# Weighted sum of gathered expert rows: from TensorE products with diagonals to scaled additions on VectorE

## What is computed

```
q  = (hx @ wq)                                   # 8 heads x 2 halves x 64
s1, s2 = scores of both halves against 128 keys each; top 16 of each; best 16 of the 256 sums
gate = softmax over the 16 chosen of a head
eid  = index of the chosen expert rows
act  = gelu(einsum('td,thkd->thk', hx, u[eid]))   # one dot product per slot
out  = einsum('thk,thkd->td', gate * act, v[eid]) # weighted sum of 128 rows of V per token
```

## Time and profile before

| what | us |
|---|---|
| median of 3 runs | 5882.7 (5859.87 to 5891.56) |
| span of the profiled execution, first to last instruction | 5620.3 |
| what lies around the span, median less span | 262.4 |
| five pair passes, first gather issue to the end of the last add to X | 743.4, 736.6, 736.2, 749.2, 739.1 |
| busy in the span: TensorE | 4119.9 (73%) |
| busy: VectorE | 3021.2 (54%) |
| busy: ScalarE | 954.0 (17%) |
| busy: GpSimd | 3143.7 (56%) |

### The profile page before, as it was taken

The page is one execution under the profiler, slowest core; times in us unless marked ns, Lnnn a source line. Parts: engine busy times, 40 slices in busy tenths (PEclk is TensorE's granted clock), DMA queues, the critical chain, the costliest instruction groups (busy, mean ns, idle before and its releaser), DMA issues. The chain is left out here.

```text
span 5620.3 us, 37241 instructions
## 1 busy us (share of the span) xinstructions
PE 4119.9 (73%) x10909; PEld 1832.8 (33%) x10909; DVE 3021.2 (54%) x6541; ACT 954.0 (17%) x2298; POOL 3143.7 (56%) x2740
## 2 busy tenths in 40 slices
PE   7986777677776677775778779677846777576766
PEld 2533554322222222322223235345512222222222
DVE  1129652765663765655646521575366466465663
ACT  0012350111111111111111110234011111111111
POOL 0005302377776777776777730240167777677775
PEclk9998898899999899998999999789979999899999
DMA  7100101499998999998999951011179999899998
GB/s 274 53 16 8 18 25 64 153 383 368 395 364 346 386 372 398 389 376 326 379 396 390 365 190 60 8 17 41 42 264 355 378 362 364 316 370 365 381 355 337
DMA packets 459025, 1468.37 MB, mean 261 GB/s; under 512 B 58966, under 2 KB 97066, under 8 KB 458818
## 3 DMA queue, kind: packets, MB, share of 16 engines
q0 software_dynamic: 368640, 1342.34, 62.7%
q1 hardware_dynamic: 81548, 116.43, 6.3%
q10 hardware_dynamic: 8634, 7.14, 0.4%
HBM read 1459.62 MB, written 6.13 MB: 261 GB/s over the span
## 5 line engine op out<-in xcount | busy, mean ns | idle before, releaser
L1530 PE MATMUL tile_acc<-peer_V,peer_diag 128*128 128x512 f32 x5120 | 2490.5, 622 | 736.6 <-DMA peer_V<-in_peer_v_dram,peer_expert 695.8
L1551 DVE CUSTOM_DVE_ANT_0 peer_U<-peer_U,peer_h 128x1024 f32<-128x1024 f32 x1280 | 1543.8, 1225 | 1377.8 <-DMA peer_U<-in_peer_u_dram,peer_expert 1373.1
L1463 POOL DMA_INDIRECT peer_U<-in_peer_u_dram,peer_expert x1280 | 1389.4, 1085 | 643.5 <-issue 526.3
L1469 POOL DMA_INDIRECT peer_V<-in_peer_v_dram,peer_expert x1280 | 1446.3, 1130 | 402.9 <-issue 271.4
L1530 PEld LDWEIGHTS tile_acc<-peer_V,peer_diag 128*128 128x128 f32 x5120 | 923.4, 195 | 2282.3 <-issue 1441.4
L1505 ACT ACTIVATE peer_diag<-small,peer_w 128x128 f32<-128x128 f32 x1280 | 493.0, 401 | 2365.2 <-PE tile_acc L1530 2139.2
L338 PE MATMUL proj_acc<-proj_w,HT 128*128 128x512 f32 (+2 forms) x1280 | 481.7, 538 | 2.9 <-DVE PR L366 2.9
L1348 PE MATMUL tile_keys<-peer_sub,peer_q 64*128 64x128 f32 x320 | 46.5, 435 | 374.8 <-DVE peer_rest L1364 294.2
L338 PEld LDWEIGHTS proj_acc<-proj_w,HT 128*128 128x128 f32 x1280 | 242.8, 190 | 235.0 <-issue 217.4
L660 POOL MEMSET glascore_Q<- 128x8192 f32 x2 | 13.8, 6925 | 539.7 <-POOLq L100 539.7
L1200 POOL TENSOR_TENSOR X<-X,out_part 128x512 f32<-128x512 f32 x20 | 25.3, 1266 | 470.6 <-DVE out_part L1190 470.6
(11 more groups left out here) (250 smaller groups left out, 3381.2 us busy)
## 6 DMA issues: line engine op xcount, KB each, us to landing
setup_ada<-in_ada_w_dram SPq DMA_DIRECT2D x12, 2048.0 KB, 16.9
peer_ada<-in_ada_w_dram SPq DMA_DIRECT2D x24, 1024.0 KB, 12.5
proj_w<-in_w_in_dram SPq DMA_DIRECT2D x10, 2048.0 KB, 7.9
peer_U<-in_peer_u_dram,peer_expert POOLq DMA_INDIRECT x1280, 6.5
peer_V<-in_peer_v_dram,peer_expert POOLq DMA_INDIRECT x1280, 6.6
out_w<-in_w_out_dram SPq DMA_DIRECT2D x2, 4096.0 KB, 14.9
query_w<-in_peer_wq_dram SPq DMA_DIRECT2D x4, 2048.0 KB, 16.0
Y<-mods SPq DMA_DIRECT2D x8, 512.0 KB, 7.4
```

The lines of the kernel that those rows point to most:

```text
L1463: pool.indirect_dma_start(s.U[:, n % RING], None, u_rows, bass.IndirectOffsetOnAxis(ap=s.expert[:, n // SLOTS, n % SLOTS:n % SLOTS + 1], a ...
L1469: pool.indirect_dma_start(s.V[:, n % RING], None, v_rows, bass.IndirectOffsetOnAxis(ap=s.expert[:, n // SLOTS, n % SLOTS:n % SLOTS + 1], a ...
L1530: mm = nc.tensor.matmul(acc[:, n // SLOTS, half], s.diag[:, n % 4], s.V[:, n % RING, 512 * half:512 * half + 512], start=n % SLOTS == 0, s ...
L1551: nc.vector.tensor_tensor_reduce(out=s.U[:, n % RING], in0=s.U[:, n % RING], in1=s.h[:, n // SLOTS], scale=1.0, scalar=0.0, op0=ALU.mult, ...
```

## The change

The sum over slots is made on VectorE in SBUF. Behind the dot product of slot n stands a scaled addition for slot n - 16: `part_out = V row * weight + part_out`, with a plain scaling for the first slot of a tile. VectorE waits for each one to end before it goes on. TensorE's products, ScalarE's diagonals and the PSUM sum are gone. `add_out` now reads the SBUF sum, and the one of the first tile comes a head earlier (head 8), as the sum's only buffer is needed again from head 9. GpSimd's order and its waits have the same text, but `sums` now counts scaled additions. VectorE's loop has a round more, for the last 16.

```diff
-        s.diag = sb("diag", [P, 4, P])
...
-            acc = st.ps("acc", [P, 2, 2, 512])
...
                     for h in range(NH + 1):
                         if h % PH == PH // 2 + 1:
                             softmax_exp(nc, act, s, sems, h // PH)
-                        if h:
-                            act.wait_ge(weights, h)
-                            for n in range((h - 1) * TOPK, h * TOPK):
-                                if n >= 4:
-                                    act.wait_ge(sums, n - 3)
-                                nc.scalar.activation(s.diag[:, n % 4], m.ident, ACT.Copy, scale=s.w[:, n:n + 1]).then_inc(diags, 1)
...
-                        if h:
-                            for n in range((h - 1) * TOPK, h * TOPK):
-                                pe.wait_ge(diags, n + 1)
-                                pe.wait_ge(vg[n % RING], 16 * (n // RING + 1))
-                                for half in range(2):
-                                    mm = nc.tensor.matmul(acc[:, n // SLOTS, half], s.diag[:, n % 4],
-                                                          s.V[:, n % RING, 512 * half:512 * half + 512],
-                                                          start=n % SLOTS == 0, stop=n % SLOTS == SLOTS - 1)
-                                mm.then_inc(sums, 1)
...
+                    def weigh_row(n):
+
+                        dve.wait_ge(vg[n % RING], 16 * (n // RING + 1))
+                        dve.wait_ge(weights, n // TOPK + 1)
+                        if n % SLOTS == 0:
+                            nc.vector.tensor_scalar(s.part_out[:], s.V[:, n % RING], s.w[:, n:n + 1], None, ALU.mult).then_inc(sums, 1)
+                        else:
+                            nc.vector.scalar_tensor_tensor(out=s.part_out[:], in0=s.V[:, n % RING], scalar=s.w[:, n:n + 1],
+                                                           in1=s.part_out[:], op0=ALU.mult, op1=ALU.add).then_inc(sums, 1)
+                        dve.wait_ge(sums, n + 1)
+
                     def add_out(j):
 
-                        dve.wait_ge(sums, SLOTS * (j + 1))
-                        link(nc.vector.tensor_tensor(s.part_out[:], acc[:, j].rearrange("p a b -> p (a b)"), s.G[:], ALU.mult))
+                        link(nc.vector.tensor_tensor(s.part_out[:], s.part_out[:], s.G[:], ALU.mult))
...
-                    for h in range(NH):
+                    for h in range(NH + 1):
                         for k in range(TOPK):
                             n = h * TOPK + k
-                            dve.wait_ge(ug[n % RING], 16 * (n // RING + 1))
-                            nc.vector.tensor_tensor_reduce(out=s.U[:, n % RING], in0=s.U[:, n % RING], in1=s.h[:, n // SLOTS],
-                                                           scale=1.0, scalar=0.0, op0=ALU.mult, op1=ALU.add,
-                                                           accum_out=s.dots[:, n:n + 1]).then_inc(dots, 1)
+                            if h < NH:
+                                dve.wait_ge(ug[n % RING], 16 * (n // RING + 1))
+                                nc.vector.tensor_tensor_reduce(out=s.U[:, n % RING], in0=s.U[:, n % RING], in1=s.h[:, n // SLOTS],
+                                                               scale=1.0, scalar=0.0, op0=ALU.mult, op1=ALU.add,
+                                                               accum_out=s.dots[:, n:n + 1]).then_inc(dots, 1)
+                            if h:
+                                weigh_row(n - TOPK)
+                        if h == NH:
+                            break
...
-                        if h == PH + 1:
+                        if h == PH:
                             add_out(0)
```

More of the change, by code:

```diff
@@ L1446, in peer_tiles @@
             st.gathers = ug + vg
-            h_now, dots, gelus, weights, diags, sums, scaled = (st.sem(x) for x in (
-                "hnow", "dots", "gelus", "weights", "diags", "vsums", "scaled"))
+            h_now, dots, gelus, weights, sums = (st.sem(x) for x in ("hnow", "dots", "gelus", "weights", "vsums"))
             adas, rows_in, modded, added, stored = (st.sem(x) for x in ("adas", "rowsin", "modded", "added", "stored"))
```

## The result

The changed kernel takes 6069.8 us, the median of 4 runs (6068.0 to 6074.2). The kernel before, run beside it, takes 5887.1 (4 runs, 5859.9 to 5892.8). The ratio is 1.0326, with a 95% interval from 1.0298 to 1.0354: slower by 183 us. The forecast was 6105 and +223.

What follows compares the result with a forecast made beforehand. Gather issues bound the kernel before, VectorE the changed one: 770.5 + 15 = 785.5 us a pass, +44.6, over five passes +223; span about 5843 plus 262.4 outside gives 6105 us, range 6010 to 6270.

Steps and rivals of the forecast that it cites:

- What bounds before: Expert passes: 512 gather issues at 1.40 us, 717 of 740.9 us, bound the pass; dot products hold issues to 1.99.
- What is removed: Per pass: 256 ScalarE diagonals and 1024 TensorE matmuls go, and with them VectorE's end wait of 29.2 us.
- a lower clock at the start of the next stage: TensorE's first products after the expert stage may start at the lower clock: nothing to a few us, taken as nothing.
- VectorE's sum: VectorE's work in one pass: 770.5 us, with 240 slots of 2.46; above 740.9, so +148 us over five passes.
- The dry ring: Gathered rows run out in heads 5 to 8 and 13 to 15: 15 us a pass, between 0 and 49.
- Issues that average more than 1.10 us: Sign expected in the profile after: GpSimd's mean gather issue longer than 1.10 us.
- The count of openings: GpSimd gets 3 issues in 2 slots or 5 in 3, needing 2 per slot; lead shrinks 0.17 to 0.25 slots.
- The time around the span: Outside the profiled span: 262.4 us of the median run, left as they are and added to 5843.
- Rival 1 (full lock): GpSimd caught at every turn, VectorE at 2.76 a slot: 842.5 a pass, +508, about 6390 us; chance 0.12.
- Rival 2 (slot 2.59): Dot product doesn't overlap its successor, slot 2.59: 802 us a pass, +305, about 6190 us; chance 0.14.
- Rival 3 (own wait free, not slower): VectorE's wait behind each addition costs nothing, slot 2.35: 742 us a pass, +6, about 5890 us; chance 0.08.
- The threshold of 2.37: From a VectorE slot of about 2.37 us down, rival 3 decides: the kernel is not slower.

Runs made afterwards that it cites:

- the second occasion: Both kernels unchanged, run again: the kernel before 5601.2 us, the changed kernel 5785.1 us against 5589.3, ratio 1.0336.
- the third pair of profiles: Both kernels unchanged, a third time: changed kernel 5782.4 us against 5594.2, ratio 1.0335; kernel before 5602.1 us in one run.
- the version with both edits: Changed kernel with the running sum in PSUM and VectorE's wait moved ahead of the next addition: 5786.9 us, ratio 1.0272 to the kernel before.
- quarter rows: Changed kernel with gathers of 256 columns of each row instead of 1024, same instructions: 5833.9 us in one run, buffer clearing included.
- the sum in PSUM: Changed kernel with the running sum in PSUM instead of SBUF, wait behind each addition kept: 5796.5 us against 5628.4 for the kernel before, ratio 1.03.
- the changed kernel's second profile: Changed kernel unchanged, profiled when run again beside the kernel before: passes of 774.3 us; timed median 5785.1 us, ratio 1.0336.
- the late wait: Changed kernel with VectorE's wait for its addition moved ahead of the next addition, behind a dot product: 5859.5 us, ratio 1.0487 to the kernel before.

## Why the prediction was right, and where it was not

The forecast was slower, by 223 us, through a VectorE that becomes the bound. Measured: slower by 183 us in the result and by 196 on the second occasion, and the second occasion's trace shows VectorE 97% busy in a pass. What the prediction did not see is how close the second bound stays: two issues take 2.49 us and VectorE's slot 2.46. Step by step:

- **What bounds before: right.** The gather issues, and the bar that dot products put on them. The wait behind each dot product, which costs VectorE time and gives GpSimd pauses, took 143 us off. With it falls a sentence from ahead of the prediction, that the engines meet only through semaphores: here a VectorE instruction holds a GpSimd issue with no semaphore between them.
- **What is removed: right, as far as shown.** The wait of 29.2 us is gone. That TensorE's and ScalarE's work was otherwise off the pace is not tested by itself; it follows from VectorE's sum, which leaves 3.8 us of the pass unexplained. Outside the passes there are 5792.1 - 3871.5 = 1920.6 us, against 5581.7 - 3671.3 = 1910.4: 10 us more. But the third pair of profiles gives 4 us more, and the first pair (that of the rows ahead of the prediction and that of the result) 11 less, so nothing is seen there of a lower clock at the start of the next stage, which the prediction took as nothing.
- **VectorE's sum: right.** 770.5 us without friction, 774.3 measured. Dot product 1.15, scaled addition 1.28 long and 1.31 with its wait, slot 2.46, all as written; the mean slot is 2.47, because of the 1.30 us that an addition takes when it gives way, which is 240 x 0.01 = 2.4 us of the 3.8.
- **The dry ring: wrong, and this is the step that failed.** It was a term of 15 us a pass. "Issues that average more than 1.10 us" were 0.98 and 0.99, and VectorE waits for no row once head 0 is done. The 15 us a pass don't exist. The count of openings took a late issue to be a missed one. That the sum still came near has two small reasons: friction was 3.8 us, and the kernel before was at 734.3 a pass where the prediction had 740.9 (44.6 - 15 + 3.8 + 6.6 = 40.0). In the trace VectorE gives way by some 0.02 us and the two stay in step at 2.49. The lower bound of the step, 0, was the value. Its mechanism is real: taking the pause away (a slot of 2.37) brought it back, at 46 us a pass on average.
- **The time around the span: wrong.** 262 us were carried as a constant, and the span and the time of one execution differ by 2 us. What differed was the occasion, as far as the runs show. It did little harm to a ratio, and only by luck little to the absolute time: the profile of after holds 58 us a pass of stops that nothing in the prediction foresaw, 290 us in all, against the 262 carried over.
- **Rival 1 (full lock): fell.** It needed 2.76 a slot; 2.47 was measured. The first issue behind a search is held (1.74 us), and in all about 31 of a pass's 512 by more than 0.1 us.
- **Rival 2 (slot 2.59): fell.** The addition starts 1.15 after the dot product.
- **Rival 3 (own wait free, not slower): fell, twice.** The wait costs the 0.11 us a slot that the prediction gave it, so the kernel is slower. And a slot of 2.37 does not make it "not slower" either: it gave 5859 against 5603. The threshold of 2.37 counted VectorE alone and left out that GpSimd can't issue two gathers in that time. The rule of the Trainium skill that a semaphore costs nothing, which the prediction set beside this rival (VectorE: DVE Perf Modes, "The DRAIN you can't avoid"), is not borne out here: from an addition to the next dot product it is 1.31 us with the wait between them (1991.26 to 1992.57), mostly 1.20 to 1.24 in the version where the wait comes later, and 1.19 in the version with both edits (2001.81 to 2003.00).

The cause of the stops in the first profile stays open. Shown is only that they lie in VectorE's idle time, where rows lay ready or none were needed, and that they were absent from four later profiled runs of the changed kernel's schedule (unchanged twice, with more waits twice), and from those with quarter rows and with the sum in PSUM. Since the kernel before was slower in those runs by as much (5887 against 5603, 284 us; the changed kernel 6070 against 5785, 285), the ratio stands without them.

## What to carry to other kernels

Before moving work to an engine with room, write down its whole chain for one unit of work; a VectorE that was 59% busy in a pass (435 of 741 us) had no room for 254 more instructions of 1.31 us (333 us). Then ask who lives in the pauses between its instructions: here a wait that looked like pure loss let the gathers through, moving it away cost 61 to 74 us, and adding one to the kernel before gave 143 us. And lay a profiled execution's span beside its own time before calling any difference overhead.

## What the runs showed of the hardware that was not expected

- VectorE and GpSimd settle into step. The one that comes late holds the other only 0.02 to 0.03 us (additions of 1.30 us in place of 1.28), so issues kept 0.94 us where a full bar gives 1.99. In the changed kernel's second profile this is so for all 780 issues that began within 0.1 us of an addition's start.
- One gather queue gives a row set of 128 x 4 KB per 1.24 to 1.245 us, and in no profile here is one faster than 1.24, whatever VectorE does: 0.94 and 0.30 between two. With quarter rows it is the same, so the bytes don't set it.
- Waits that are already met cost VectorE nothing here: four more per slot in the text, two more semaphore instructions in its queue, 5785.2 us against 5785.1.
- A VectorE instruction with two 128x1024 SBUF inputs holds an issue that begins 0.1 to 0.9 us into it (70 of 70 into additions, and 120 of 120 with the late wait); with one of them in PSUM it doesn't (0 of 75, and 0 of 109 with the late wait).
- VectorE can stand still for 1 to 2 us, at times up to 5, between instructions on its own tiles, some 58 us a pass in one execution and none in the others.
- TensorE's granted clock stays at 0.50 to 0.53, its 1.2 GHz level, through passes in which it is busy for 36 us of 774; what that costs behind the passes is lost in the scatter named above (11 us less to 10 us more outside the passes).
